# Encoder step on one core: retention projections by tile in turns, sample scores by head pairs, convolution transposes in other PSUM banks, bias products moved

## The chip, the cores and the metric

One core of a Trainium2 chip runs the whole program in one launch. Its engines work side by side and wait for each other on semaphores: TensorE (PE, matmuls and transposes into PSUM, which has eight banks; PEld is its loading of the stationary operand), VectorE (DVE), ScalarE (ACT), GpSimd (POOL), and SyncE (SP), whose queue issues most DMAs. The metric is the device time of one execution in microseconds (us).

## The reference, cut to what matters

Two layers work on 512 prompt rows and 32 sample rows of width 1024, all in float32. Each layer is cut here to what the change touches:

```
for l in range(2):
    a_q, a_k, a_v, r_q, r_k, r_v, r_g, c_in = split(x @ w_in[l])
    A: softmax attention in pairs (two maps of 64 per head, 4 heads) on 512 prompt keys,
       bias[h, key_pos - query_pos] from a 32-bucket table;
       the 32 sample rows attend to 1024 cached keys and their own 32
    B: rq, rk = rotary(r_q), rotary(r_k)          # 4 heads of 64
       ro = ((rq @ rk.T) * decay) @ r_v + (rq * d) @ state
       out = rms_norm(ro) * silu(r_g)
    C: u = c_in[:256] * sigmoid(c_in[256:]); depthwise causal convolution of width 31,
       layer norm, silu; the last 30 rows of u are an output
    x = LN(alpha * x + concat(A, B, C) @ w_out[l])
    x = LN(alpha * x + top2_of_16_experts(x)); x = x + sigmoid(x @ Wg) * (p[l] @ Wp)
```

The keys a_k of all rows are outputs too.

## The kernel before

Each engine has one instruction stream, in an order written out by hand; semaphores couple them. Rows are held in five tiles t (four of 128 prompt rows, one of 32 sample rows). Weights pass through a ring of six 1 MB slots that SP fills in the order of a list; a slot is loaded again when TensorE has counted the products that read it. A function bank_plan gives each use of a PSUM bank a key and a bank, round robin: `room(key)` waits until the bank's last user has been read out, `turned(key)` waits until this key's own result has been read out.

TensorE's order in a layer, with lines of the profile:

- In layer 0 alone: four matmuls on a tile of ones (L901), whose result nobody reads, the transposes of x tile 0 (L887), then `bias_products` (L897): three products of a 32-row bucket table with the bias table, 4 output rows each. ACT copies them (L1497) and stores them by DMA; POOL later spreads them over DRAM and loads the two bias tiles, for which DVE waits before its convolution.
- The value projection (L922), eight 128-row chunks for each tile; behind chunk 5 of a tile come the transposes of the next tile.
- Three projections with features on the partitions (L950), the transposes of the keys to token rows (ktok, L961, copied by ACT into the memory of rvg, from which a DMA stores them), then, when DVE's convolution is done, its transposes (convT, L970, copied by ACT at L1522) and those of its last rows (tail, L975, copied by DVE). Before the attention TensorE waits for `turned(tail)` and `turned(convT 4)`.
- The attention in 19 steps u. Step u computes two score matrices of unit u (L994, banks 0 and 1, read by DVE at L1919), half a tile of a retention projection (L1009, eight passes), the transposes of the probabilities of unit u-2 (L1021) and the product with the values of unit u-3 (L1031). The halves come from the list PIECES: all five tiles of group 3 (rotary queries and keys, bank 2), then all five of group 4 (values and gates, bank 3). The first half of a next tile waits until the last tile's bank has been read: `g_used[3]` comes from the fourth product of DVE's `rotate` (L1860 to L1863), `g_used[4]` from ACT's copy (L1552), which for tile 0 first waits until the key rows are stored.
- The retention: transposes of the rotated rows (L1051), inner products `inside(t)` (L1066, two banks, b = partitions 0 to 63 and 64 to 127, two heads q in each), state updates (L1108), transposes of cached keys `turn_cache(h)` (L1082), copied by ACT (L1576) into one of two buffers, then by tile the products with the state (L1131, b and q again), with the values (L1141), and the transposes of the convolution's rows (L1092).
- The sample scores: for each head h, on two halves n of the cache and two maps m2 (partitions 0 to 63 and 64 to 127), products of 32 sample queries with 512 cached keys (L1156, output rows 32h to 32h+31 of bank 2*m2+n) and with the 32 own keys (L1159). Heads 2 and 3 use the buffers of heads 0 and 1 again:

```python
                for h in range(H):
                    sample_scores(h)
                    if h + 2 < H:
                        turn_cache(h + 2)
```

- Transposes of the retention's rows (L1092), the output projection (L1206), the router, and the experts in a loop over rounds (L1343, L1344, L1370, L1371), whose weights SP streams.

Of the kernel before, what the change touches and what calls it, by code (L numbers as in the profile page):

```python
# [20 lines left out]
P = 128  # L21
# [35 lines left out]
GROUPS = (2, 5, 0, 1, 3, 4)  # L57
PIECES = [(g, t, half) for g in (3, 4) for t in range(TILES) for half in range(2)]
ATT_STEPS = 4 * 4 + 3
# [21 lines left out]
LOGIT_BANK = 4  # L81
BIAS_BANK = (4, 5, 6)
PLP_AT = (4, 1, 2, 3, 0)
# [3 lines left out]
def bank_plan():  # L87
# [7 lines left out]
    keys += [("ktok", t) for t in range(TILES)]  # L95
    keys += [("convT", t) for t in range(TILES)] + [("tail",)]

# [27 lines left out]
    for key in keys + late:  # L125
        if key == ("logit",):
            held, b = True, LOGIT_BANK
        elif key in placed:
            b = placed[key]
        else:  # L130
# [83 lines left out]
def encoder_step(nc, a, o, c):  # L214

    ctx = ExitStack()
    with ctx:
# [652 lines left out]
        def _(pe):  # L870
# [27 lines left out]

            pe.wait_ge(hw_zero, 1)
            for n in range(4):  # L900
                pe.matmul(bank[7][:, 0:4 * P], ones[:], ones[:].unsqueeze(1).to_broadcast([P, 4, P]), start=True, stop=True)  # L901
            pe.wait_ge(ident_bias, 16)

            for l in range(DEPTH):

                if l == 0:
                    turn_tile(l, "x0", x_ready, 0)
                    bias_products()
                for t in range(TILES):
# [8 lines left out]
                    for kc in range(KC):  # L918
# [62 lines left out]

                turned(l, ("tail",))
                turned(l, ("convT", 4))
                n_att = len(UNITS_ATT)
                for u in range(ATT_STEPS):
                    if u < n_att:
                        i, h = UNITS_ATT[u]
# [67 lines left out]
                def inside(t):  # L1055
                    for b in range(2):
                        key = ("ri", t, b)

                        if b == 0 and use(key) != use(("rqkT", t)):
                            turned(l, ("rqkT", t))  # L1060
                        room(l, key)
                        if t == 4:
                            pe.sem_inc(pe_pass, 1)
# [4 lines left out]
                        m.then_inc(full[use(key)], 1)  # L1068

# [52 lines left out]
                for t in range(TILES):  # L1122
                    state = t if t < 4 else 5
                    for b in range(2):
                        key = ("rc", t, b)
                        room(l, key)
                        r = slice(HD * b, HD * b + HD)
                        if t == 4:
                            pe.sem_inc(pe_pass, 1)
                        for q in range(2):  # L1130
                            m = pe.matmul(B(key)[0:ROWS[t], q * HD:(q + 1) * HD], rqkT[r, q, span(t)], rst[r, state, q, :], start=True, stop=True)  # L1131
                        m.then_inc(full[use(key)], 1)
                        last_on[use(key)] = key
                    key = ("ro", t)
# [13 lines left out]

                def sample_scores(h):
                    hs = slice(DEC * h, DEC * h + DEC)  # L1150
                    for n in range(2):
                        pe.wait_ge(ck_done[n], H * l + h + 1)
                        pe.sem_inc(pe_pass, 1)
                        for m2 in range(2):
                            r = slice(HD * m2, HD * m2 + HD)
                            pe.matmul(bank[2 * m2 + n][hs, :], qT[r, h, SEQ:TOK], kcT[r, h % 2, n * 512:(n + 1) * 512], start=True, stop=True)  # L1156
                    for m2 in range(2):
                        r = slice(HD * m2, HD * m2 + HD)
                        m = pe.matmul(bank[4 + 3 * m2][hs, 0:DEC], qT[r, h, SEQ:TOK], kT[r, h, SEQ:TOK], start=True, stop=True)  # L1159
                    m.then_inc(ss_full, 1)  # L1160

                for h in range(H):
                    sample_scores(h)
                    if h + 2 < H:
                        turn_cache(h + 2)

# [291 lines left out]
        def _(sc):  # L1458
# [17 lines left out]
            for l in range(DEPTH):  # L1476
# [855 lines left out]
```

## Time and profile before

| | us |
|---|---|
| median of the runs | 1498.93 (1498.40 to 1505.48, 3 runs) |
| the profiled execution's own time | 1506.39 |
| span of its trace | 1504.6 |
| TensorE busy in it | 1427.7 (95%) |
| VectorE busy | 601.4 (40%) |
| ScalarE busy | 276.7 (18%) |

The span runs from the first to the last instruction of the program; the own time has 1.79 us around it. Matmuls are pipelined, so that a row of several matmuls ends later than the next one starts, and starts are the better measure. Layer 0 runs from 0 to about 779 us, layer 1 repeats its order about 756 us later. A float32 matmul stands in the trace as two passes, each with its own weight load; "x8" counts passes.

### The profile page before, as it was taken

How to read it: one execution, taken by the hardware profiler on the slowest of the kernel's cores; microseconds unless marked ns; L12 is line 12 of the kernel's file. 1: busy time of each engine (PE TensorE's matmuls, PEld its weight loads, DVE VectorE, ACT ScalarE, POOL GpSimd, SP SyncE). 2: the span in 40 equal slices, each digit the busy share in tenths (PEclk: the TensorE clock that was granted, in tenths of full speed). 3: DMA queues.
4: the chain of work that ended last, by engine and by line, in shares of the span. 5: the costliest groups of instructions: out<-in, count | busy, mean ns of one | idle time of the engine just before them, and what ended most of it. 6: DMA issues, size and time to landing. Idle time of an engine off the chain costs nothing.

```text
span 1504.6 us, 20579 instructions
## 1 busy us (share of the span) xinstructions
PE 1427.7 (95%) x6978; PEld 739.5 (49%) x6978; DVE 601.4 (40%) x1224; ACT 276.7 (18%) x671; POOL 118.4 (8%) x137
## 2 busy tenths in 40 slices
PE   8999999999799999998999999999988999999898
PEld 3787446554234444443456874465543444433344
DVE  5086774444401101115550777744544101101366
ACT  1201245212100000001121112452121100000112
POOL 2100000110000000003000000001100000000300
PEclk8999999899899999998999999999999999999999
DMA  9614011344479999957031131113434899999821
GB/s 294 257 64 160 6 56 60 140 183 143 141 313 426 427 426 427 393 223 278 23 126 59 56 130 45 56 60 141 186 141 141 317 427 426 427 427 427 329 86 46
DMA packets 80940, 319.47 MB, mean 212 GB/s; under 512 B 12684, under 2 KB 15044, under 8 KB 56300
## 3 DMA queue, kind: packets, MB, share of 16 engines
q1 hardware_dynamic: 66772, 272.19, 46.2%
q0 software_dynamic: 9280, 29.68, 5.4%
q10 hardware_dynamic: 4824, 16.75, 2.8%
q8 instruction: 38, 0.62, 0.2%
q14 instruction: 26, 0.21, 0.0%
HBM read 429.21 MB, written 29.67 MB: 305 GB/s over the span
## 4 chain that ended last, share of the span: by engine, by line
PE 82%; DVE 5%; DMA 5%; issue 2%; ACT 2%; SPq 1%; DVEq 1%; POOL 1%; ACTq 0%; POOLq 0%
PE psum L1343 18%; PE psum L950 12%; PE psum L1370 9%; PE psum L1009 8%; PE psum L1423 8%; PE psum L1206 7%; PE psum L922 4%; DMA region<-in_w_exp_up_dram 3%; PE psum L887 2%; PE psum L1344 2%; PE psum L866 1%; PE psum L1257 1%; PE psum L1322 1%; PE psum L994 1%; DMA region<-in_w_exp_down_dram 1%
## 5 line engine op out<-in xcount | busy, mean ns | idle before, releaser
L1343 PE MATMUL psum<-ring,xT 128*64 128x512 f32 x800 | 356.1, 597 | 10.5 <-DMA region<-in_w_exp_gate_dram 5.3
L1344 PE MATMUL psum<-region,xT 128*64 128x512 f32 x800 | 356.9, 598 | 0.0
L1343 PEld LDWEIGHTS psum<-ring,xT 128*64 128x64 f32 x800 | 107.6, 138 | 211.8 <-issue 211.7
L1370 PE MATMUL psum<-ring,region 128*64 128x512 f32 x400 | 178.0, 597 | 4.1 <-issue 2.5
L1371 PE MATMUL psum<-region 128*64 128x512 f32 x400 | 178.1, 597 | 0.0
L950 PE MATMUL psum<-xT,ring 128*128 128x272 f32 x768 | 176.5, 393 | 0.0
L950 PEld LDWEIGHTS psum<-xT,ring 128*128 128x128 f32 x768 | 145.8, 190 | 30.1
L2214 DVE COPY region<-psum 128x512 f32<-128x512 f32 x23 | 15.9, 691 | 322.5 <-PE psum L1371 322.5
L1009 PE MATMUL psum<-ring,xT 128*128 128x512 f32 (+1 forms) x288 | 134.2, 609 | 7.2 <-DVE region L1863 7.2
L1423 PE MATMUL psum<-ring,xT 128*128 128x512 f32 x256 | 116.7, 611 | 1.5 <-issue 1.5
L773 POOL TENSOR_TENSOR rr<-rq,half 128x1 f32<-128x1 f32 (+4 forms) x41 | 56.8, 1386 | 738.1 <-DVE rq L1729 277.8
L1370 PEld LDWEIGHTS psum<-ring,region 128*64 128x64 f32 x400 | 54.7, 138 | 108.4 <-issue 108.4
L1344 PEld LDWEIGHTS psum<-region,xT 128*64 128x64 f32 x800 | 107.6, 138 | 0.0
L1813 DVE SCALAR_TENSOR_TENSOR region<-region,hwT 128x574 f32<-128x574 f32 x120 | 92.5, 813 | 4.9 <-issue 0.4
L1009 PEld LDWEIGHTS psum<-ring,xT 128*128 128x128 f32 (+1 forms) x288 | 49.8, 183 | 76.5 <-issue 63.8
L2204 DVE TENSOR_TENSOR region<-region,psum 128x512 f32<-128x512 f32 x25 | 17.2, 688 | 158.1 <-PE psum L1344 158.1
L1423 PEld LDWEIGHTS psum<-ring,xT 128*128 128x128 f32 x256 | 49.2, 196 | 62.1 <-issue 59.8
L1465 ACT ACTIVATE region<-psum 128x512 f32<-128x512 f32 (+5 forms) x74 | 35.3, 521 | 155.8 <-PE psum L961 60.3
L1465 ACT ACTIVATE xT<-psum 128x512 f32<-128x512 f32 (+1 forms) x60 | 29.6, 532 | 183.6 <-PE psum L887 183.3
L1206 PE MATMUL psum<-ring,region 128*128 128x512 f32 x128 | 58.6, 600 | 1.4 <-ACT region L1602 0.7
L922 PE MATMUL psum<-ring,xT 128*128 128x512 f32 x128 | 59.0, 613 | 0.0
L1206 PE MATMUL psum<-ring,xT 128*128 128x512 f32 x128 | 57.5, 592 | 0.0
(288 smaller groups left out, 1491.0 us busy)
## 6 DMA issues: line engine op xcount, KB each, us to landing
region<-in_w_exp_gate_dram SPq DMA_DIRECT2D x54, 1024.0 KB
ring<-in_w_exp_gate_dram SPq DMA_DIRECT2D x54, 1024.0 KB
region<-in_w_exp_up_dram SPq DMA_DIRECT2D x54, 1024.0 KB
ring<-in_w_exp_up_dram SPq DMA_DIRECT2D x54, 1024.0 KB
ring<-in_w_exp_down_dram SPq DMA_DIRECT2D x54, 1024.0 KB
region<-in_w_exp_down_dram SPq DMA_DIRECT2D x54, 1024.0 KB
ring<-in_w_in_dram SPq DMA_DIRECT2D x24, 1024.0 KB, 9.1
expert_results<-region ACTq DMA_DIRECT2D x23, 512.0 KB, 7.7
```

Source lines behind the costliest of these rows:

```text
L773: pl.tensor_tensor(rr[:, at:at + cols], rq[:, at:at + cols], half[:, 0:cols], ALU.pow).then_inc(root_got, 1)
L922: m = pe.matmul(B(key)[0:ROWS[t], :], xT[:, kc, span(t)], slot(u)[:, kc % 4, :], start=kc == 0, stop=kc == KC - 1)
L950: m = pe.matmul(B(key)[:, 0:HALF], w, xT[:, kc, half * HALF:(half + 1) * HALF], start=kc == 0, stop=kc == KC - 1)
L1009: m = pe.matmul(bank[g - 1][0:ROWS[t], :], xT[:, 4 * half + kc, span(t)], slot(w)[:, kc, :], start=half == 0 and kc == 0, stop=half == 1 a ...
L1206: m = pe.matmul(B(key)[0:ROWS[t], :], mixT[kc][:, span(t)], slot(u)[:, kc % 4, :], start=kc == 0, stop=kc == KC - 1)
L1343: pe.matmul(bank[b][front, :], xeT[:, kc, front], ring[:, BLOCK_SLOT[u], kc % 4, :], start=kc == 0, stop=kc == KC - 1)
L1344: m = pe.matmul(bank[b][last, :], xeT[:, kc, last], back[:, UNIT_ROOM[u], kc % 4, :], start=kc == 0, stop=kc == KC - 1)
L1370: pe.matmul(bank[5 + half][front, :], hT[:, 2 * n + q, front], ring[:, BLOCK_SLOT[u], 2 * q + half, :], start=n + q == 0, stop=n + q == 2)
L1371: m = pe.matmul(bank[5 + half][last, :], hT[:, 2 * n + q, last], back[:, UNIT_ROOM[u], 2 * q + half, :], start=n + q == 0, stop=n + q == 2)
L1423: m = pe.matmul(B(key)[0:ROWS[t], :], xT[:, kc, span(t)], slot(u)[:, kc % 4, :], start=kc == 0, stop=kc == KC - 1)
L1465: sc.activation(dst, src, func).then_inc(free[use(key)], 1)
L1813: m = ve.scalar_tensor_tensor(cT[:, s, :], src, hwT[:, s, 32 + j:33 + j], cT[:, s, :], ALU.mult, ALU.add)
```

## The change

Seven edits, all of order or place; no product is added, and four are left out.

- The four matmuls on ones and TensorE's wait ahead of them are gone.
- `bias_products` moves from ahead of the value projection of tile 0 to behind chunk 5 of it, after the transposes of tile 1; its banks are 5, 6, 7 instead of 4, 5, 6; ACT's copies and DMAs, and TensorE's wait for the copies, move one tile later.
- The transposes of the convolution use banks 4, 5, 6, 7, 4 and the tail bank 5 (before: 4, 5, 6, 7, 0 and 1). Six empty places in the plan keep all later banks as they were.
- The wait for them ahead of the attention is split: step 0 waits for ktok 1 to 3, step 1 for ktok 4, step 2 for convT 2 to 4 and the tail.
- The halves of the retention projections come in the order of PIECE_ORDER, groups 3 and 4 in turns. By it `rotate` stands at steps 1, 5, 9, 13, 15 (before 1, 3, 5, 7, 9), the copies of group 4 at 3, 7, 11, 17, 18 (before 11, 13, 15, 17, 18).
- `inside` and the products with the state loop over q outside and b inside, and ask for both banks first.
- Sample scores run for heads 0 and 1 together, then both cache transposes, then heads 2 and 3 together.

```diff
+PIECE_ORDER = ((3, 0), (4, 0), (3, 1), (4, 1), (3, 2), (4, 2), (3, 3), (3, 4), (4, 3), (4, 4))
+PIECES = [(g, t, half) for g, t in PIECE_ORDER for half in range(2)]
-BIAS_BANK = (4, 5, 6)
+BIAS_BANK = (5, 6, 7)
...
+    keys += [("convT", t) for t in range(TILES)] + [("tail",)] + [None] * (TILES + 1)
+    fixed = {("convT", t): (4, 5, 6, 7, 4)[t] for t in range(TILES)}
+    fixed["tail",] = 5
...
-            pe.wait_ge(hw_zero, 1)
-            for n in range(4):
-                pe.matmul(bank[7][:, 0:4 * P], ones[:], ones[:].unsqueeze(1).to_broadcast([P, 4, P]), start=True, stop=True)
...
-                    bias_products()
...
-                            if l == 0 and t == 0:
+                            if l == 0 and t == 1:
                                 pe.wait_ge(bias_row, 3)
                             turn_tile(l, "x0", x_ready, t + 1)
+                            if l == 0 and t == 0:
+                                bias_products()
...
-                turned(l, ("tail",))
-                turned(l, ("convT", 4))
...
+                    if u == 0:
+                        for t in range(1, 4):
+                            turned(l, ("ktok", t))
+                    elif u == 1:
+                        turned(l, ("ktok", 4))
+                    elif u == 2:
+                        for t in range(2, 4):
+                            turned(l, ("convT", t))
+                        turned(l, ("convT", 4))
+                        turned(l, ("tail",))
...
-                        for q in range(2):
+                    for q in range(2):
+                        for b in range(2):
+                            key = ("ri", t, b)
                             r = slice(HD * b, HD * b + HD)
...
-                def sample_scores(h):
+                def sample_scores(pair):
                     for n in range(2):
-                        pe.wait_ge(ck_done[n], H * l + h + 1)
+                        for h in pair:
+                            pe.wait_ge(ck_done[n], H * l + h + 1)
                         pe.sem_inc(pe_pass, 1)
                         for m2 in range(2):
                             r = slice(HD * m2, HD * m2 + HD)
+                            for h in pair:
+                                pe.matmul(bank[2 * m2 + n][DEC * h:DEC * h + DEC, :], qT[r, h, SEQ:TOK], kcT[r, h % 2, n * 512:(n + 1) * 512], start=True, stop=True)
...
+                sample_scores((0, 1))
+                turn_cache(2)
+                turn_cache(3)
+                sample_scores((2, 3))
...
-                    if l == 0 and t == 0:
+                    if l == 0 and t == 1:
                         for n in range(3):
```

The products with the state are changed as `inside` is.

## Rows read from the trace of the kernel before

**Rows 1.** The page, part 1: busy time of TensorE.
```profile
PE 1427.7 (95%) x6978; PEld 739.5 (49%) x6978; DVE 601.4 (40%) x1224; ACT 276.7 (18%) x671; POOL 118.4 (8%) x137
```
**Rows 2.** Waits of TensorE, whole span: us in total, times, longest.
```profile
PE psum L1009 <- DVE region L1863: 7.2, 6, 2.0
...
PE psum L1343 <- DMA region<-in_w_exp_gate_dram: 5.3, 5, 2.1
...
PE psum L1156 <- DVE region L1977: 1.9, 1, 1.9
PE psum L1131 <- ACT region L1576: 1.8, 2, 0.9
```
**Rows 3.** Timeline of the start: start, length, engine, line, idle before and its releaser.
```profile
1.58 6.12 PE L901 MATMUL psum<-ones 128*128 128x512 f32 x8 [1.58 <-POOL history_and_tail_rows L779]
10.13 1.94 PE L887 MATMUL psum<-ident,x 128*128 128x128 f32 x8 [2.43 <-issue]
12.00 4.10 PE L897 MATMUL psum<-region 32*4 32x512 f32 x6
12.11 0.60 ACT L1465 ACTIVATE xT<-psum 128x512 f32<-128x512 f32 x1 [0.26 <-PE psum L887]
16.03 7.44 PE L922 MATMUL psum<-ring,xT 128*128 128x512 f32 x12
24.18 7.03 PE L922 MATMUL psum<-ring,xT 128*128 128x512 f32 x16
```
**Rows 4.** Landing of the first two weight loads, issued at 2.1 and 3.4.
```profile
DMA to landing us min/median/max: 9.2/10.5/11.9
```
**Rows 5.** Stretches: length, busy PE, PEld, DVE, ACT, POOL, granted clock, DMA, GB/s.
```profile
9.90:20.14 10.24, 10.01 (x19) 4.01 (x20) 6.79 (x12) 2.67 (x5) 2.34 (x2) 0.50 1.06 338
...
258.00:273.02 15.02, 14.69 (x90) 12.50 (x91) 7.98 (x25) 1.77 (x5) 2.27 (x1) 0.54 0.04 8
...
1012.20:1022.80 10.60, 8.65 (x90) 7.44 (x90) 7.85 (x25) 1.77 (x5) 2.27 (x1) 1.00 0.05 12
```
**Rows 6.** Waits of DVE between 50 and 140 us.
```profile
DVE region L1794 <- PE psum L950: 14.7, 2, 13.7
```
**Rows 7.** Timeline between the convolution and the attention, layer 0.
```profile
143.22 2.36 ACT L1522 ACTIVATE region<-psum 128x256 f32<-128x256 f32 x5
...
143.45 0.60 PE L975 MATMUL psum<-ident,region 128*30 128x128 f32 x4
...
145.72 0.49 PE L994 MATMUL psum<-region 64*128 64x128 f32 x4 [1.67 <-ACT region L1522]
```
**Rows 8.** Timeline of DVE: a rotation (step 1), and the scores of step 14.
```profile
155.63 0.42 DVE L1860 TENSOR_TENSOR region<-psum,rot 128x256 f32<-128x256 f32 x1 [1.74 <-PE psum L1009]
...
156.63 0.41 DVE L1863 TENSOR_TENSOR region<-psum,rot 128x256 f32<-128x256 f32 x1
...
221.35 1.22 DVE L1919 SCALAR_TENSOR_TENSOR region<-psum,bias_p 128x1024 f32<-128x1024 f32 x1 [1.13 <-PE psum L994]
```
**Rows 9.** Timeline of the sample scores: layer 0, then two short cuts of layer 1.
```profile
276.46 1.09 PE L1082 MATMUL psum<-ident,ring 128*128 128x128 f32 x8
277.15 1.09 ACT L1576 ACTIVATE region<-psum 128x512 f32<-128x512 f32 x2 [4.16 <-PE psum L1082]
...
283.20 0.66 PE L1092 MATMUL psum<-ident,region 128*128 128x128 f32 x4
...
1027.41 1.05 PE L1156 MATMUL psum<-region 64*32 64x512 f32 x4
...
1031.22 1.06 PE L1156 MATMUL psum<-region 64*32 64x512 f32 x8
```
**Rows 10.** Weight loads of the sample scores: ns min/median/max, first and last start.
```profile
L1156 PEld LDWEIGHTS psum<-region x64: 103/107/174, 273.0 to 1032.1; 64*32 64x32 f32 x64
```
**Rows 11.** Storing of the last key rows: issue, and DMA (KB, us to landing).
```profile
143.63 0.37 SPq L647 DMA_DIRECT2D out_new_k_sample_dram<-region  x1
...
out_new_k_sample_dram<-region SPq DMA_DIRECT2D x1, 64.0 KB, 8.4
```

More of the change, by code:

```diff
@@ L57 @@
 GROUPS = (2, 5, 0, 1, 3, 4)
-PIECES = [(g, t, half) for g in (3, 4) for t in range(TILES) for half in range(2)]
+PIECE_ORDER = ((3, 0), (4, 0), (3, 1), (4, 1), (3, 2), (4, 2), (3, 3), (3, 4), (4, 3), (4, 4))
+PIECES = [(g, t, half) for g, t in PIECE_ORDER for half in range(2)]
 ATT_STEPS = 4 * 4 + 3
@@ L95, in bank_plan @@
     keys += [("ktok", t) for t in range(TILES)]
-    keys += [("convT", t) for t in range(TILES)] + [("tail",)]
+    keys += [("convT", t) for t in range(TILES)] + [("tail",)] + [None] * (TILES + 1)
+    fixed = {("convT", t): (4, 5, 6, 7, 4)[t] for t in range(TILES)}
+    fixed["tail",] = 5
     keys += [("rqkT", t) for t in range(TILES)]
@@ L129, in bank_plan @@
             b = placed[key]
+        elif key in fixed:
+            b = fixed[key]
         else:
@@ L976, in _ @@
                 m.then_inc(full[use(("tail",))], 1)
-                turned(l, ("tail",))
-                turned(l, ("convT", 4))
                 n_att = len(UNITS_ATT)
+                assert [use(("ktok", t)) for t in range(TILES)] == [7, 0, 1, 2, 3]
                 for u in range(ATT_STEPS):
+                    if u == 0:
[8 more added lines that the diff above has]
+                        turned(l, ("tail",))
                     if u < n_att:
@@ L1061, in inside @@
                         room(l, key)
-                        if t == 4:
-                            pe.sem_inc(pe_pass, 1)
-                        for q in range(2):
+                    if t == 4:
+                        pe.sem_inc(pe_pass, 1)
+                    for q in range(2):
+                        for b in range(2):
+                            key = ("ri", t, b)
                             r = slice(HD * b, HD * b + HD)
@@ L1067, in inside @@
                                           start=True, stop=True)
-                        m.then_inc(full[use(key)], 1)
+                            if q == 1:
+                                m.then_inc(full[use(key)], 1)
                 def turn_cache(h):
@@ L1124, in _ @@
                     for b in range(2):
[L1125 to L1130, printed above, removed]
+                        room(l, ("rc", t, b))
+                    if t == 4:
+                        pe.sem_inc(pe_pass, 1)
+                    for q in range(2):
+                        for b in range(2):
+                            key = ("rc", t, b)
+                            r = slice(HD * b, HD * b + HD)
                             m = pe.matmul(B(key)[0:ROWS[t], q * HD:(q + 1) * HD], rqkT[r, q, span(t)], rst[r, state, q, :], start=True, stop=True)
-                        m.then_inc(full[use(key)], 1)
-                        last_on[use(key)] = key
+                            if q == 1:
+                                m.then_inc(full[use(key)], 1)
+                                last_on[use(key)] = key
                     key = ("ro", t)
@@ L1147, in _ @@
                     turned(l, last_on[b])
-                def sample_scores(h):
-                    hs = slice(DEC * h, DEC * h + DEC)
+                def sample_scores(pair):
                     for n in range(2):
-                        pe.wait_ge(ck_done[n], H * l + h + 1)
+                        for h in pair:
+                            pe.wait_ge(ck_done[n], H * l + h + 1)
                         pe.sem_inc(pe_pass, 1)
@@ L1155, in sample_scores @@
                             r = slice(HD * m2, HD * m2 + HD)
[L1156 to L1165, printed above, removed]
+                            for h in pair:
+                                pe.matmul(bank[2 * m2 + n][DEC * h:DEC * h + DEC, :], qT[r, h, SEQ:TOK], kcT[r, h % 2, n * 512:(n + 1) * 512], start=True, stop=True)
+                    for h in pair:
+                        for m2 in range(2):
+                            r = slice(HD * m2, HD * m2 + HD)
+                            m = pe.matmul(bank[4 + 3 * m2][DEC * h:DEC * h + DEC, 0:DEC], qT[r, h, SEQ:TOK], kT[r, h, SEQ:TOK], start=True, stop=True)
+                        m.then_inc(ss_full, 1)
+                sample_scores((0, 1))
+                turn_cache(2)
+                turn_cache(3)
+                sample_scores((2, 3))
                 pe.wait_ge(ret_done, l + 1)
```

## The prediction, made before the change was run

> **What bounds the kernel now.** I read the page first: TensorE is busy 95% of the span [rows 1]. A gain has to come from TensorE's stream: fewer gaps, matmuls that overlap better, or more clock. So the second view is the list of what TensorE waited for [rows 2]. Of its entries the change touches four: the retention projections that wait for DVE's rotation (7.2 us over both layers, six waits), the wait ahead of the attention (1.67 us in layer 0 [rows 7]), and two at the retention's products. The third view is the timeline around each edited place [rows 3, 7 to 9], the fourth the granted clock by stretch [rows 5]. There the reader sees that the same 90 passes of the retention take 15.02 us in layer 0 at a mean clock of 0.54 and 10.60 us in layer 1 at 1.00.
>
> **The start.** The matmuls on ones end at 7.70. TensorE then sits idle for 2.43 us, and its clock is at 0.50, the 1.2 GHz level, from 9.90 to 20.14 [rows 3, 5]. Nothing after 10.13 waits for them; I price their removal at 0. Before, the bias products take 12.00 to 16.03 at half clock. Now the projection can follow the copy of the transposed tile, which ends at 12.71, so at about 12.8. Its weights have landed at 11.3 (first half, 2.1 + 9.2) and 15.3 (second half, first needed after eight passes; 3.4 + 11.9) [rows 4]. Before, the clock rose 4.1 us after the projection began. I assume the same delay, so the twelve passes and the transposes again last 8.15 us (16.03 to 24.18) and end at 20.95. The bias products follow at full clock, in half of their 4.03 us: 23.0, where before the projection went on at 24.18. Gain 1.2. Bounds: if the clock rises at 20.14 whatever TensorE does, eight and a half of the twelve passes run at half clock (about 0.86 each, 0.43 after), and the point comes at 24.5, a loss of 0.3; if it rises sooner, at most 1.8 gained. TensorE's own wait for ACT's copies of them moves one tile on, and comes about 5 us after they can be done; ACT's copy of the first value tile now stands behind these copies, and its bank is not wanted again for several tiles. Both 0. The bias table goes to DRAM some 8 us later than before. What waits for it is DVE, ahead of the convolution, and DVE has 13.7 us of waiting for TensorE soon after [rows 6], so I count 0; a delay beyond that cover would cost its excess one for one.
>
> **Convolution transposes and the start of the attention.** Before, TensorE idles 1.67 us until ACT's fifth copy. Now the fifth transpose uses bank 4, so a new wait stands in TensorE's stream, for ACT's first copy, and the tail waits for the second. The copies take 2.36 / 5 = 0.47 each from 143.22, so the tail can start at about 144.26 instead of 143.45 and ends 0.60 later, at 144.86. Behind these waits only the attention's first scores are queued, and they follow at once: 145.72 - 144.86 = 0.9 gained in each layer. The moved waits for copies of steps 1 and 2 come 4 and 8 us later, when the five copies (done at 145.58) are long over: 0. Bounds: 0 (ACT later than here) to 1.67.
>
> **Projections in turns.** With the groups alternating, the next tile of a bank comes two steps later, and DVE's rotation ends long before. The six waits of 7.2 us go, 3.6 a layer. What is late next: tiles 3 and 4 of group 3 stand next to each other, and the rotation of tile 3 now falls into step 13, where its score rows are longest (128x1024). DVE comes free there at 221.35 - 1.13 = 220.22; four rotation products take 1.41 (155.63 to 157.04) [rows 8], so the bank is free at about 221.7, and TensorE is through with the scores of step 14 at about 221.3. I count a new wait of 0.4: 3.2 gained in each layer. Bounds: 2.4 (the wait also delays the next step) to 3.6. Tiles 3 and 4 of group 4 stand as before. The weights of group 3 are counted read at step 15 instead of 9, so SP loads the cached values six steps later, near 230 (step 14 is at 221.35). Behind that hold SP has only loads that wait for the last products of group 4 anyway, and the cached values are first needed after the sample scores, which end at 283.2 [rows 8, 9]: 50 us of cover, so 0, and the excess if a load took longer than that.
>
> **Row halves side by side.** In layer 1 TensorE already finishes the retention early and waits 1.9 us for DVE; ahead of these products it waits for ACT's copy, 0.9 in each layer [rows 2]. Whatever a better overlap of halves gives goes into these waits; asking for both banks first costs nothing for the same reason. I count 0. Bounds: if TensorE sets the pace, as in layer 0 at half clock, the L1131 passes there could give up to 1 us; otherwise 0.
>
> **Sample scores.** Two cuts of equal length show the new overlap already: while one head runs, four passes fill 1.05 us; where head 3 follows head 2 without a cache transpose between them, eight passes fill 1.06 [rows 9]. So a pass of 512 columns costs one slot of 0.43, shared by two maps or by two maps and two heads. Before, from the transposes of head 2 to the first row transpose, 283.20 - 276.46 = 6.74. Now, from the same point: ACT's copies start 0.69 in and take 0.55 each (1.24, 1.78). The transposes of head 3 have no scores in front of them any more, so each half waits for a copy; they start at 1.34 and 1.88, and their copies end at 2.58 and 3.13. The paired scores start at 2.68, take four slots to 4.40, and their own-key products end at about 4.6. Gain 6.74 - 4.6 = 2.1 a layer; the first pair takes as long as head 0 alone did. Bounds: if only two passes ran at a time, the first pair would cost 1.7 more and the second end at 6.3, a loss of 1.3; without the waits for ACT the gain would be 2.8.
>
> The Trainium skill ("TensorE: Matmul & The Clock Gate", Part 3, The mechanism) says that a weight load overlaps a matmul in flight only when the row group differs, and the two heads of a pair share theirs. By it, eight loads of 0.107 us [rows 10] would stand free in each pair, four pairs in all, and the gain summed below would shrink by 3.4. The cut with eight passes shows no room for that, so the trace so far speaks against the rule and I do not take it.
>
> **Sum.** Each layer 0.9 + 3.2 + 2.1 = 6.2, two layers 12.4, the start 1.2: 13.6. Nothing between these places and the end keeps its own time: the loads of the expert stage are released by TensorE's progress. On the profiled execution's own time: 1506.39 - 13.6 = 1492.8. That execution is 7.46 above the median, and its stretch at half clock explains 15.02 - 10.60 = 4.42 of that. I therefore take the median as an execution without that stretch and subtract from it: 1498.93 - 13.6 = 1485.3.
>
> **Rivals.** (1) *The clock takes part of it back.* The gaps that go were ahead of the attention, but the sample scores get new ones, and the retention fell to half clock in one layer and not in the other at the same order. For it: the passes and DVE's busy time (7.98 and 7.85) were alike in both layers [rows 5], so little decides. Against: the median seems free of it. If one layer has that stretch in most executions, 1485.3 + 4.4 = 1489.7; if both, 1494.1. (2) *Only two passes overlap*, because the pair writes one bank where heads 2 and 3 had used four: 2 x (2.1 + 1.3) = 6.8 back, 1492.1. Against it stands the cut with eight, though on other banks. (3) *The weight loads stand free*, 1485.3 + 3.4 = 1488.7. (The rule of the Trainium skill named above.) (4) *The expert stage absorbs the gain*: TensorE waits 5.3 us there for weights [rows 2]. If the stream of weights had a start of its own, the end would not move: 1498.9. Against: it starts on TensorE's own counts. (5) *Slower: the key rows.* ACT's first copy of group 4 overwrites the key rows and now waits for their store at step 3 instead of 11. The last store lands at about 143.6 + 8.4 = 152.0 [rows 11]. Step 3 comes four steps of about 4 us after 145.7, so ACT is there at about 161: 9 us of cover. A later store would hold ACT, two steps on TensorE, in both layers. It would decide from (13.6 + 7.5) / 2 + 9 = 19.6 us of lateness on, and gives 1506.4 or more.
>
> **Chances and range.** The forecast 0.60; clock in one layer 0.15, in both 0.05; two passes only 0.07; free loads 0.04; absorbed 0.06; slower 0.03. Within 0.5% (7.5 us, about what a measurement of this kernel tells from no change) of 1498.93 means 1491.4 to 1506.4. Faster: 0.60 + 0.15 + 0.04 = 0.79; same: 0.05 + 0.07 + 0.06 = 0.18; slower 0.03. Low end: all upper bounds, 1.8 + 2 x (1.67 + 3.6 + 2.8) = 17.9, and 1 for the row halves: 1480.0. High end: the clock in both layers. So 1480.0 to 1494.1.
>
> **What would show it.** Right: no wait of L1009 for L1863 except near 0.4 at step 14; about 0.8 idle among the convolution transposes and none before L994; sixteen L1156 passes in about 1.9 us; 4.6 us from the transposes of head 2 to the row transposes; the first L922 near 12.8 and its clock up near 17. Wrong: L1156 in slots of four passes, a clock of 0.5 after the sample scores or over the retention in both layers, ACT waiting for a store at step 3, or an expert stage longer by what the front saved.

## The result, and the profile after

The changed kernel took 1484.66 us (median of 1481.60, 1494.21, 1487.73 and 1480.05); beside it the kernel before took 1498.40 to 1505.48 (a fourth execution, of 2122.24, is left out). The ratio is 0.9901, with a 95% interval of 0.9874 to 0.9928. The forecast was 1485.3, or a ratio of 0.9909, and "faster". A second measurement with twelve executions (below) gives 0.9928 [0.9903, 0.9954], so the first one was on the lucky side, and why the two differ became the main question. In both, the interval lies clear of 1.

The profiled execution of after took 1481.6, its span 1479.8. The page's part 1, beside [rows 1]:

```profile
PE 1404.2 (95%) x6970; PEld 727.9 (49%) x6970; DVE 601.0 (41%) x1224; ACT 275.6 (19%) x671; POOL 117.9 (8%) x137
```

The share is the same 95%, with 23.5 us less of busy time: eight passes of ones fewer, passes that overlap better, and passes at a better clock. Idle time as a whole went only from 76.9 to 75.6: the rotation's waits went, but the start, without the ones, idles longer. Waits of TensorE after, to set beside [rows 2]:

```profile
PE psum L1362 <- DMA region<-in_w_exp_gate_dram: 4.0, 6, 1.7
PE psum L1174 <- DVE region L1996: 3.6, 2, 2.0
...
PE psum L1147 <- ACT region L1595: 1.9, 2, 1.0
...
PE psum L1021 <- DVE region L1882: 0.6, 2, 0.3
```

The rotation's six waits of 7.2 have become two of 0.3. The wait ahead of the sample scores now shows in both layers; [rows 2] had it in one, since in the other layer the retention ran at half clock and DVE was never late. Now the timeline at the edited places, first the start ([rows 3]):

```profile
10.01 1.94 PE L892 MATMUL psum<-ident,x 128*128 128x128 f32 x8 [10.01 <-DVE x L1770]
12.68 7.62 PE L923 MATMUL psum<-ring,xT 128*128 128x512 f32 x12 [0.73 <-issue]
20.14 1.04 PE L892 MATMUL psum<-ident,x 128*128 128x128 f32 x8
21.11 2.15 PE L902 MATMUL psum<-region 32*4 32x512 f32 x6
23.18 3.27 PE L923 MATMUL psum<-ring,xT 128*128 128x512 f32 x7
```

The eight transposes at 10.01 take the 1.94 of [rows 3], where the clock stood at 0.50, and the first passes of the projection start 0.85 apart up to 17.08 and 0.43 apart from 17.57 on. So TensorE began at half clock here too, although the record of the granted clock says 1.00 (length, busy PE, granted clock, DMA, GB/s):

```profile
9.00:12.60 3.60, 1.94 (x8) 1.00 1.05 408
```

Next the convolution's transposes ([rows 7]), the one new wait at step 14 ([rows 8]) and the sample scores ([rows 9]), all in layer 0:

```profile
141.46 1.04 PE L973 MATMUL psum<-ident,region 128*128 128x128 f32 x8
142.74 0.39 PE L973 MATMUL psum<-ident,region 128*32 128x128 f32 x2 [0.24 <-ACT region L1541]
143.24 0.61 PE L978 MATMUL psum<-ident,region 128*30 128x128 f32 x4
143.78 0.49 PE L1006 MATMUL psum<-region 64*128 64x128 f32 x4
...
213.95 3.62 PE L1021 MATMUL psum<-ring,xT 128*32 128x512 f32 x8 [0.30 <-DVE region L1882]
...
261.31 1.92 PE L1174 MATMUL psum<-region 64*32 64x512 f32 x16 [1.66 <-DVE region L1996]
263.02 0.27 PE L1178 MATMUL psum<-region 64*32 64x32 f32 x8
263.22 1.09 PE L1097 MATMUL psum<-ident,ring 128*128 128x128 f32 x8
264.57 1.15 PE L1097 MATMUL psum<-ident,ring 128*128 128x128 f32 x8 [0.25 <-ACT region L1595]
265.96 1.92 PE L1174 MATMUL psum<-region 64*32 64x512 f32 x16 [0.24 <-issue]
267.67 0.27 PE L1178 MATMUL psum<-region 64*32 64x32 f32 x8
267.87 0.66 PE L1107 MATMUL psum<-ident,region 128*128 128x128 f32 x4
```

Sixteen passes of a pair fill 1.92, as eight of one head did: they start in groups of four within 0.05 us, 0.43 apart (261.31 to 261.33, then from 261.74, 262.17 and 262.60), and the loads for a group run while the group before it is under way. And from the transposes of head 2 (263.22) to the row transposes (267.87) it is 4.65, where 6.74 stood. Last, the starts that bound the stretches in the table below: the keys' transposes of layer 0, then of layer 1 the first scores of the attention, the transposes of the rotated rows and the sample scores, before and after.

```profile
140.15 2.37 PE L961 MATMUL psum<-ident,region 128*128 128x128 f32 x20 [0.58 <-DVE region L1836]
...
901.82 0.49 PE L994 MATMUL psum<-region 64*128 64x128 f32 x4 [1.66 <-ACT region L1522]
...
1000.19 2.30 PE L1051 MATMUL psum<-ident,region 128*128 128x128 f32 x20 [0.82 <-ACT region L1531]
...
1022.86 2.88 PE L1156 MATMUL psum<-region 64*32 64x512 f32 x8 [1.95 <-DVE region L1977]
```
```profile
139.25 2.37 PE L964 MATMUL psum<-ident,region 128*128 128x128 f32 x20 [0.58 <-DVE region L1855]
...
881.59 0.49 PE L1006 MATMUL psum<-region 64*128 64x128 f32 x4
...
976.47 2.30 PE L1063 MATMUL psum<-ident,region 128*128 128x128 f32 x20 [0.81 <-ACT region L1550]
...
999.37 2.85 PE L1174 MATMUL psum<-region 64*32 64x512 f32 x16 [1.97 <-DVE region L1996]
```

The sum's terms, measured by starts in both traces (after minus before; layer 1 where layer 0 of before ran at half clock):

| term | forecast | measured |
|---|---|---|
| start, once (24.18 to 23.18, in this pair) | -1.2 | -1.0 |
| convolution to attention, a layer (5.57 to 4.53) | -0.9 | -1.04 |
| attention with the projections, layer 1 (98.37 to 94.88) | -3.2 | -3.49 |
| retention up to the sample scores, layer 1 (22.67 to 22.90) | 0 | +0.23 |
| sample scores, layer 0 (6.74 to 4.65) | -2.1 | -2.09 |
| sum, with two layers | -13.6 | -1.0 - 2 x 6.39 = -13.8 |

The start's -1.0 belongs to this pair of executions and not to the change. Over the nine profiles with the new start and no ones ahead of it, the same point comes between 22.32 and 24.27, and the 24.27 is the changed kernel itself, run again; in the three with the old start it comes at 24.18, 24.16 and 22.61. It depends on when the clock rises, so no gain or loss of the start is shown. The other terms repeat: with the edit in question, at full clock and without fillers, the three stretches are 4.53, 94.88 and 4.65 in every profile, within 0.02.

The span itself is 24.8 shorter. The other 11 fit the clock: the mean clocks of the two executions, 0.977 and 0.988, stand for 34.6 and 17.8 us of lost clock time, and 5.1 of the 34.6 lie in the start of before. What differs is the retention of layer 0 at half clock before ([rows 5]) and not after, 1.7 at the head of the attention, and shorter stretches, most in the expert stage, that fall elsewhere in each execution.

### The profile page after: what moved, and what is told of

Its sections match the earlier page's. It is cut to its first block, busy times and chain, and to the rows that moved or that the text cites. A ratio compares the mean times of both kernels' runs of the same rounds, so it can differ in the third digit from the quotient of the medians.

```text
span 1479.8 us, 20569 instructions
## 1 busy us (share of the span) xinstructions
PE 1404.2 (95%) x6970; PEld 727.9 (49%) x6970; DVE 601.0 (41%) x1224; ACT 275.6 (19%) x671; POOL 117.9 (8%) x137
## 4 chain that ended last, share of the span: by engine, by line
PE 79%; DMA 7%; DVE 5%; issue 3%; SPq 2%; ACT 2%; DVEq 1%; POOL 0%; ACTq 0%; POOLq 0%
PE psum L1362 17%; PE psum L953 12%; PE psum L1389 9%; PE psum L1442 8%; PE psum L1021 8%; PE psum L1225 7%; PE psum L923 4%; DMA region<-in_w_exp_up_dram 3%; PE psum L892 2%; PE psum L871 1%; PE psum L1363 1%; PE psum L1276 1%; PE psum L1341 1%; PE psum L1006 1%; SPq L709 1%
```

## The experiments

**Sample scores head by head again** (one head at a time in the old loop).

```diff
-                sample_scores((0, 1))
-                turn_cache(2)
-                turn_cache(3)
-                sample_scores((2, 3))
+                for h in range(H):
+                    sample_scores(h)
+                    if h + 2 < H:
+                        turn_cache(h + 2)
```

> The changed kernel with the sample scores head by head again, a cache transpose after heads 0 and 1. If the pairs give what was forecast, the time from the transposes of head 2 to the first transpose of the retention's rows goes from 4.65 us back to 6.7 in a layer at full clock, and nothing else in the layer moves. If the gain at this place came from the clock (layer 0 of the profiled kernel before ran part of it at half clock), the time at full clock stays near 4.7.

1491.75. Layer 0, timeline from the second head on:

```profile
264.99 1.91 PE L1173 MATMUL psum<-region 64*32 64x512 f32 x8
...
266.89 1.09 PE L1097 MATMUL psum<-ident,ring 128*128 128x128 f32 x8
267.92 1.94 PE L1173 MATMUL psum<-region 64*32 64x512 f32 x12
```

Eight passes of one head again take the 1.91 that sixteen took in pairs. From the transposes of head 2 to the row transposes it is 7.54 here, with the first transposes at half clock; with the old order at full clock (the kernel before with fillers, below) it is 6.74 in both layers. The pairs are worth 2.1 a layer. The rivals of two passes at a time and of free-standing weight loads fall. The Trainium skill ("TensorE: Matmul & The Clock Gate", Part 3, The mechanism) lists that a weight load overlaps a matmul in flight only where the row group differs, though the same section also names a background weight buffer as a place that a load can go to ahead of time; with the prediction's eight free loads a pair would take about 0.86 longer than 1.92, and it doesn't. The measurement decides.

**Projections by group again.**

```diff
-PIECES = [(g, t, half) for g, t in PIECE_ORDER for half in range(2)]
+PIECES = [(g, t, half) for g in (3, 4) for t in range(TILES) for half in range(2)]
```

> The changed kernel with the five tiles of group 3 ahead of the five of group 4 again. If the waits for the rotation were the gain, L1021 waits for DVE's rotation six times, 7 us in both layers together, and the attention, from the first scores to the transposes of the rotated rows, takes 98.4 us in each layer at full clock, against 94.9. If DVE's order sets the pace in another way, the waits come back but the attention grows by less than 2 us a layer.

1503.25, one execution, with the retention of layer 0 at half clock. The rotation's waits are back to the digit:

```profile
PE psum L1021 <- DVE region L1882: 7.2, 6, 2.0
```

From the attention's scores to the retention it takes 100.10 and 100.07 in the two layers, 5.2 more than after. Of that 3.5 are the waits, and 1.7 are clock: each layer has a short stretch at half clock inside its attention, which after has not. Windows of the same stretch, this run and then after (length, busy time of PE, granted clock, DMA, GB/s):

```profile
170.00:180.00 10.00, 8.02 (x22) 0.83 0.00 0
```
```profile
170.00:180.00 10.00, 10.00 (x38) 1.00 0.01 2
```

**Convolution transposes in the old banks, one wait ahead of the attention.**

```diff
+                turned(l, ("tail",))
+                turned(l, ("convT", 4))
```

> The changed kernel with the old banks of the convolution's transposes and the old wait ahead of the attention. If the new banks gave the gain, TensorE idles 1.67 us ahead of the first scores, and from the first transpose of the keys to the first scores it takes 5.57 us instead of 4.53: 1.0 a layer, 2.1 in all. If DVE's copy of the last rows decides when the attention gets going, the first scores come later but DVE's first addition comes at the same distance, and the attention is shorter by as much.

1490.86, one execution, with the waits back: from the keys' transposes to the first scores it takes 5.57 and 5.56, 1.04 a layer more than after. The attention of layer 0 still takes 94.88, so DVE's copy of the last rows does not decide when it gets going. Layer 1 has the short stretch at half clock in its attention (1.7):

```profile
PE psum L993 <- ACT region L1528: 3.3, 2, 1.7
```

**Row halves in the old order**, run once and later timed.

```diff
-                    for q in range(2):
-                        for b in range(2):
+                    for b in range(2):
+                        for q in range(2):
```

> The changed kernel with the retention's products in the old order of halves. By my forecast this edit is worth nothing: from the transposes of the rotated rows to the sample scores 22.7 us either way at full clock. A rival from the trace after: asking for both banks first makes tile 4's products wait 0.5 us for VectorE, and the stretch is 22.9 with the edit and 22.66 without it. If the halves overlap only with the edit, it is longer than 23.5 without it.

> The changed kernel with the row halves of the retention's products in the old order (all products of a half together, each bank asked for where it is used). The prediction counted 0 for this part. If the new order costs the 0.24 us by which one layer's retention was longer at equal clock, the old order gains 0.2 to 0.5 us in all, which these times cannot show; if side by side saved up to 1 us a layer, it loses 2. If the old order drops the retention to half clock (both layers in its one look), its median is 4 to 9 us above that of the changed kernel; if that was chance, the two medians lie within about 3 us.

The first took 1494.49, its retention at half clock in both layers, which looked like a cost of the old order. The timed run says no: 1488.69 (nine executions, 1479.46 to 1496.78), ratio 0.9912 [0.9884, 0.9941], not to be told from the changed kernel's 0.9928. In its profile the retention's products run at full clock in both layers: from the rotated rows to the sample scores 22.52 and 22.67, against 22.65 and 22.90 after. So the new order, side by side with both banks asked for first, costs 0.13 and 0.23 and gives nothing. After shows the waits that go with it: 0.52 and 0.30 for DVE's rst, where before has 0.16 in one layer.

**The changed kernel again.**

> The changed kernel itself, once more. Theory A (the spread of its times comes from stretches at half clock that fall or don't fall on an execution, each of the retention's costing about 4.4 us in one layer): times spread between about 1480 and 1494, and the mean granted clock of each execution goes with its time, about 1 us for each 0.001 of clock (1480.05 at 0.989, 1494.21 at 0.976 so far). Theory B (the spread has another source): time and clock do not go together. The median against the kernel before: 0.990 by the first measurement, 0.991 by the prediction's sum.

1490.16 (twelve executions, 1479.25 to 1497.83). Five with a mean clock of 0.975 to 0.977 took 1494.24 to 1497.83, five at 0.980 to 0.982 took 1486.72 to 1491.20, two at 0.987 and 0.988 took 1479.25 and 1480.12. Time and clock go together, some 1.3 us for each 0.001 of mean clock. The kernel before, twenty executions beside these: fourteen at 0.980 to 0.983 (1499.72 to 1505.04), two at 0.988 (1493.56 and 1494.14). At equal clock the change is worth 1493.85 - 1480.12 = 13.7 at 0.988, and 1502.26 (median of nine) - 1488.56 = 13.7 at 0.981. Take the two equal numbers with care. Each rests on one execution of the changed kernel, and those at 0.980 to 0.982 spread over 4.5 us. And the mean clock is not the same measure in both kernels: the profiles with the old start record 6.83 to 10.24 us at half clock there, 0.002 to 0.003 of the mean, and those with the new start record none, though their first passes stand 0.85 apart as well. With that counted, the difference at equal clock would be some 3 to 4 us larger. Nor does half clock cost the same everywhere: 3.41 us of it cost 1.7 in the attention, 17.07 us some 6 in the retention and the first sample scores of before. So the mean clock is a coarse measure.

**Fillers**: products of ones that nobody reads, in a bank that is free, ahead of the waits at the attention's end, in the retention and ahead of the sample scores (with a wait for the tile of ones at the start, not shown here).

```diff
+            def fill(b, n):
+                for _ in range(n):
+                    pe.matmul(bank[b][:, 0:2 * P], ones[:], ones[:].unsqueeze(1).to_broadcast([P, 2, P]), start=True, stop=True)
...
+                fill(0, 3)
                 pe.wait_ge(oT_done, 4 * l + 3)
...
+                fill(0, 2)
                 rows_out(pe, l, 3)
+                fill(0, 2)
...
+                room(l, ("rc", 0, 0))
+                fill(use(("rc", 0, 0)), 3)
                 pe.wait_ge(conv_act, TILES * (l + 1))
...
-                for b in (1, 2, 3, 4, 7, 0):
+                for b in (4, 7, 0):
                     turned(l, last_on[b])
+                fill(0, 4)
+                for b in (1, 2, 3):
+                    turned(l, last_on[b])
```

> Leaves nothing of the computation out; adds products of ones, never read, in places where TensorE waits: three before the attention's last row copy, two before and two after the last output transposes, three before the convolution's activation, four before the sample scores, each of 256 columns (half of a 0.45 us product of 512 columns, so about 0.22 each, 0.5 to 0.9 in gaps of 0.5 to 1.7). Theory A (the granted clock of the retention follows from how busy TensorE is in the stretch ahead of and in it): the retention stays at full clock in both layers, the spread narrows, and the median falls by about 3 to 6 us against the changed kernel. Theory B (half clock there is chance that the kernel's order does not govern): still at half clock in about half of the stretches, the median equal or up to 2 us higher, since some of the products run past their gaps.

1482.04 (1478.27 to 1485.90, clock 0.986 to 0.992), ratio 0.9880 [0.9855, 0.9905]. The retention of layer 0 by windows, first the changed kernel again, then with fillers:

```profile
251.00:260.00 9.00, 8.11 (x56) 0.70 0.07 14
260.00:272.00 12.00, 11.69 (x74) 0.51 0.00 1
```
```profile
251.00:260.00 9.00, 9.00 (x88) 1.00 0.07 15
260.00:272.00 12.00, 10.64 (x93) 1.00 0.33 105
```

In the same 9 us TensorE gets through 88 passes instead of 56. The fillers cost about 0.6 from the rotated rows to the output projection in layer 0 (32.35 against 31.72 after) and 0.33 in the attention, at whose end the first three stand (95.21 against 94.88); they return more. A filler of 256 columns takes 0.43, two passes, twice what was expected of it, so some run past their gaps. Over the ten profiles without fillers, twelve retentions of twenty had over 13 us at half clock; over the three kernels with all fillers, none of six.

**Fillers ahead of the retention's products only.**

> Leaves nothing out; only the seven fillers ahead of the attention's last copy and around the last output transposes, without those ahead of the convolution's activation and ahead of the sample scores. Theory A (the fall is decided by the thin stretch between the attention's end and the retention's first products): as good as with all fillers, 1478 to 1486, no long stretch at half clock. Theory C (decided by the gaps inside the retention's products and ahead of the sample scores): half clock stays, about 1488 with a spread of 14. In between, if both contribute.

1491.84, ratio 0.9943 [0.9922, 0.9964]: no help. What TensorE did before the clock fell, timeline of layer 0:

```profile
250.09 0.32 PE L1090 MATMUL psum<-region 64*32 64x32 f32 x8 [0.52 <-DVE rst L1991]
250.33 1.09 PE L1107 MATMUL psum<-ident,ring 128*128 128x128 f32 x8
252.42 0.66 PE L1160 MATMUL psum<-rst,region 64*128 64x64 f32 x8 [1.00 <-ACT region L1610]
...
254.27 1.12 PE L1160 MATMUL psum<-rst,region 64*128 64x64 f32 x8
```

Up to 250 there is no gap, then 0.52 and 1.00, and within 2 us of the second the same eight passes take 1.12 instead of 0.66 (granted clock 0.5 from 254.31 on). In layer 1 the clock fell only later, for 3.41 us from 1012.06 on, in the sample scores. So the fillers at the attention's end do not hold the clock by themselves; what the run with all fillers has in addition are those in the two later gaps. Whether these two alone would do was not run, and the same gaps in layer 1 of this profile had no long fall behind them.

**Fillers in the kernel before.**

> Leaves nothing out; the kernel before the change with the same products of ones in the same gaps as in the run with fillers. With both orders held at full clock, the change itself stands without the clock's spread. Theory A (the change is worth what the prediction's terms sum to, and the rest of what the medians show is the clock): times near 1493 to 1497, about 13.6 us above the changed kernel with fillers (1482.04), and no stretch at half clock over the retention in either layer. Theory B (the change gained partly because it changed how often the clock falls): the distance is well under 13, or the half-clock stretches stay.

1498.85 (twelve executions, 1492.57 to 1504.74), ratio 0.9985 [0.9968, 1.0002], above the 1493 to 1497 that were expected. Retention at full clock in both layers, from the transposes of head 2 to the row transposes 6.74 in both, but both attentions with their short stretch at half clock. Against the changed kernel with fillers: 0.9985 - 0.9880 = 0.0105 of 1500, or 15.8, give or take 4.5 by the two intervals. By their rows the two profiles differ by 16.2 without the start: the sum's 12.8 without its start, and 1.7 a layer for the clock of the attention. That short stretch stands in six of the eight attentions with the old projections or the old banks, and in none of twenty with both edits.

Its start, though it is the old one, differs from [rows 3]. Here the clock was still up behind the ones and an idle 3.10, fell at 11.86 by the record, and the projection goes on at 22.61, earlier than in eight of the nine profiles with the new start:

```profile
10.07 1.06 PE L887 MATMUL psum<-ident,x 128*128 128x128 f32 x8 [3.10 <-issue]
...
22.61 3.60 PE L926 MATMUL psum<-ring,xT 128*128 128x512 f32 x8
```

**Products of ones at the very start**, seven ahead of the first transposes and one behind them.

> Leaves nothing out; adds seven products of ones at the very start, ahead of the first transposes, and one between the transposes and the projection, so that TensorE has worked without a gap when the projection begins. Theory A (the half clock of the first passes is owed to the idle time in front of them): the projection's twelve first passes take about 5.2 us instead of 7.6, the bias products come 2 to 3 us sooner, and the end with them. Theory B (the clock rises at its own time after the start, whatever is done): twelve passes in about 7.6 as before, no gain. Gain by A some 2.5 us, little beside a spread of 14: the rows of the start decide it, not the median.

1484.17, ratio 0.9879 [0.9850, 0.9908]. The start's timeline:

```profile
1.57 8.19 PE L906 MATMUL psum<-ones 128*128 128x512 f32 x14 [1.57 <-POOL history_and_tail_rows L784]
10.20 1.06 PE L892 MATMUL psum<-ident,x 128*128 128x128 f32 x8 [0.43 <-issue]
11.10 1.02 PE L906 MATMUL psum<-ones 128*128 128x512 f32 x2
12.05 5.39 PE L930 MATMUL psum<-ring,xT 128*128 128x512 f32 x12
17.49 1.09 PE L892 MATMUL psum<-ident,x 128*128 128x128 f32 x8
...
20.59 7.13 PE L930 MATMUL psum<-ring,xT 128*128 128x512 f32 x16
```

Twelve passes in 5.39 instead of 7.62, and the point after the bias products 2.6 earlier than after (20.59 against 23.18) and 1.7 earlier than in any profile without these ones; in the last run below, which has them too, it comes at 20.55. The clock at the start depends on TensorE's work before it. The Trainium skill ("TensorE: Matmul & The Clock Gate", Part 1, What's actually happening) states as much, half rate by default and activity releasing it, and these rows agree: the same transposes take 1.06 here and 1.94 after. The retention fell to half clock in both layers of this profile all the same. The median is 6 us below that of the changed kernel beside it, where the rows give 2.6 against after and 3.7 against the second profile (24.27): with six executions the rest is within the clock's spread.

**The old start.**

> The changed kernel with the bias products back ahead of the first projection and the matmuls on ones back. By the rows of both traces: the first projection begins 3.3 us later, and the point where it goes on after the second tile's transposes comes 1.0 us later (24.2 instead of 23.2). If removing the matmuls on ones alone had cost clock at the start, less than 1.0.

1494.90, one execution; its retention was at half clock in both layers, so its time says little. The projection goes on at 24.16, 0.98 later than after, as expected, but earlier than the 24.27 of the changed kernel run again. So the run does not show what the start is worth, and since it puts both edits of the start back, it does not tell them apart.

```profile
16.02 7.43 PE L927 MATMUL psum<-ring,xT 128*128 128x512 f32 x12
23.28 1.04 PE L892 MATMUL psum<-ident,x 128*128 128x128 f32 x8
24.16 7.03 PE L927 MATMUL psum<-ring,xT 128*128 128x512 f32 x16
```

**All together**: fillers, ones at the start, row halves in the old order, the last projection tiles as (3, 3), (4, 3), (3, 4), (4, 4), own-key products ahead of the paired scores.

> Leaves nothing out; the changed kernel with the products of ones at the start (measured 2.6 us sooner out of the first projections), the old order of the row halves (0.13 to 0.23 us a layer shorter by rows), the last two projection tiles in the order that takes the 0.3 us wait at step 14 away, the sample scores' own-key products moved ahead of the paired scores, and the fillers in the retention. Theory A (clock held, terms add): 1482.04 - 2.6 - 2 x (0.2 + 0.3) = 1478.4, with a spread of 8 or less. Theory B (fillers and the other order disturb each other, or the start's gain is lost to the clock later): 1482 or more.

1480.00 (1475.91 to 1482.30), ratio 0.9862 [0.9840, 0.9884]. The wait at step 14 is gone, and the output projection of layer 0 starts at 268.46, 1.9 before after's and 3.2 before that of the fillers alone: 3.0 of this comes from the start (20.55 against 23.54) and 0.27 from the retention. The wait that is gone gained nothing, for the attention takes 95.23 here and 95.21 there. The median is 2.0 below the fillers alone, where 3.6 was expected, and the intervals overlap. Its interval lies clear of those of both kernels of this study.

## Why the prediction was right

- **The terms.** In this pair of traces each of the sum's five steps stands within 0.3 of what was measured, and the total within 0.2 (13.6 against 13.8). The four terms of the layers repeat in the other profiles; the start's does not. At equal mean clock the timed executions say 13.7, which agrees better than the evidence for it allows (see the changed kernel again).
- **Start.** The projection came at 12.68 where I had 12.8, and its clock rose near 17 as foreseen; the point behind the bias products came at 23.18 where I had 23.0. But "I assume the same delay" holds for one execution: in the same kernel run again the passes stood 0.85 apart up to 19.08, and the point came at 24.27, within the 0.3 of loss that I had as a bound. So the 1.2 is not shown as a gain of the change, and 1.0 of the 13.8 was the luck of this pair. The price 0 for the four ones matmuls held where the idle time behind them left TensorE at half clock [rows 3]; in one execution of three it did not (22.61). More of them, with no gap, would have been a gain of 2.6.
- **Convolution transposes.** 1.04 against 0.9. The wait for ACT, ahead of the fifth transpose, came out at 0.24 instead of 0.8, and the scores follow with no idle time.
- **Projections in turns.** 3.5 against 3.2; the new wait at step 14 was there, 0.30 against 0.4. Not foreseen: the clock of the attention, 1.7 a layer when it falls, which the old waits brought and the new order removes.
- **Row halves.** Counted 0, measured a loss of 0.13 to 0.23 a layer. The step "asking for both banks first costs nothing" failed by that much: in layer 0 the last tile of the inner products now waits 0.52 for DVE's rst, where before it waited 0.16.
- **Sample scores.** 2.09 against 2.1, step for step: four slots a pair, 4.65 against 4.6.
- **The other end.** The rival of the key rows did not happen; ACT's first copy of group 4 began at 160.34, with no wait for a store. The bias table came later too, and DVE waited 33.0 for it instead of 32.0, then 13.1 for TensorE instead of 13.7: covered, as said. The expert stage did not absorb the gain.
- **The step that failed is the base.** "I therefore take the median as an execution without that stretch." Executions of the kernel before with the highest clock take 1494, and its usual ones about 1502; 1498.93, from three, lay between. With the levels kept apart the sums are 1493.85 - 13.6 = 1480.3 for an execution near 0.988 (measured 1479.25 to 1481.60 at 0.987 to 0.989) and 1502.26 - 13.6 = 1488.7 for the usual one; the median of all sixteen of the changed kernel is 1488.85. The forecast of 1485.3 stands between the two, and so did the first median: that four executions came within 0.7 us of it was luck.
- **Rival 1 came in part.** It gave 1489.7 if one layer's retention falls in most executions. The second median, 1490.16, and the median of all sixteen lie nearer to it than to the forecast. A retention at half clock in both layers, which I had named as a sign of being wrong, stands in the second profile of this same kernel. Fillers gave the changed kernel 0.0048 of the time (7 us) and the kernel before 0.0015 (2 us, not clear of noise), so without them part of the gain may go back to the clock. Whether the new order falls more often is not shown: run beside each other, the two had mean clocks of 0.980 and 0.982, and the first leaves its start out. The gap ahead of the products with the state is 0.9 to 1.0 in both, and no run here separates the rest.

## What to carry to other kernels

Before a median is the base of a sum, ask which clock its executions had: here one retention at half clock cost 4.6 us (27.22 against 22.65), more than any edit gave in a layer at full clock, and the mean granted clock of each run told the levels apart. Look at the passes as well as at the record, which can leave a stretch out. Price a term that hangs on the clock, such as the start, from several executions and not from a pair. Price edits by rows at full clock, in the layer that has it. Where TensorE waits between thin products, a few unread products in a free bank can cost about 1 us a layer and save 7 or 8 in all, and they make the next measurement sharper too (1478.27 to 1485.90 instead of 1479.25 to 1497.83).

## What the runs showed of the hardware that was not expected

- Behind gaps of 0.5 to 1.7 us between thin products TensorE fell to its 1.2 GHz level for 13.65 or 17.07 us, in twelve retentions of twenty; with the gaps filled, the 2.4 GHz level stayed in six of six.
- The same kernel on the same chip fell or did not fall from one execution to the next: 1479.25 to 1497.83.
- At the start the clock was up before the first real product when ones ran from 1.57 to 9.4 or 9.8 and the gap behind them was 0.43 or 0.71. With fewer ones and a pause of 2.43 or 2.44 it was back at half (two executions); with a pause of 3.10 it was still full in a third and fell 1.8 later.
- The record of the granted clock can leave a stretch out: in the changed kernel it says 1.00 from the start, while eight transposes take 1.94 there and 1.04 ten microseconds later.
- Passes of 64x32 by 512 columns of two row halves and two heads ran four at a time: sixteen started in four groups, 0.43 apart.
